# A two-layer hybrid decoder kernel: other orders at its start, in the first mixer's scan and at the change of mixers

## What is computed

```python
h = concatenate([meta, x])
for i in range(2):
    if i == 0:
        h = h + gla_mixer(rms_norm(h, gla_norm), gla_w_in, gla_w_gk, gla_b_gk, gla_head_norm, gla_w_out)
    else:
        h = h + gdn_mixer(rms_norm(h, gdn_norm), gdn_w_in, gdn_conv_w, gdn_a_log, gdn_dt_bias, gdn_head_norm, gdn_w_out)
return rms_norm(h, final_norm)[:, 16:]

# gla_mixer: q, k, v, z, gk_low = split(h @ w_in); gates from gk_low
#   per chunk of 64 tokens: o = (q e^b) S + tril((q e^b)(k e^-b)^T) v ;  S = S * decay + (k e^(b_last-b))^T v
#   return (rms_norm(o, head_norm) * silu(z)) @ w_out
# gdn_mixer: h @ w_in, causal convolution, silu, l2 norm, delta rule in chunks, norm, silu gate, @ w_out
```

## Time and profile before

| | |
|---|---|
| median of 3 runs | 1481.02 us (1479.55 to 1483.16) |
| the profiled execution's own time | 1483.98 us |
| its span | 1482.2 us |
| PE busy | 1433.6 us (97%) |
| PE weight loads | 1201.6 us (81%) |
| DVE busy | 769.2 us (52%) |
| ACT busy | 454.4 us (31%) |
| POOL busy | 376.2 us (25%) |
| mean granted clock of PE | 0.997 |

### The profile page before, as it was taken

One profiled execution on the slowest core, in us unless ns is written; L12 is line 12 of the kernel. 1 busy time (PEld: TensorE's weight loads), 2 busy tenths in 40 slices (PEclk: granted clock), 3 DMA queues, 4 the chain that ended last, 5 costly groups with the idle time before them and its releaser, 6 DMA issues.

```text
span 1482.2 us, 21429 instructions
## 1 busy us (share of the span) xinstructions
PE 1433.6 (97%) x8482; PEld 1201.6 (81%) x8482; DVE 769.2 (52%) x985; ACT 454.4 (31%) x948; POOL 376.2 (25%) x303
## 2 busy tenths in 40 slices
PE   5999999999999999999999998999999999999997
PEld 4777799968788779999999998978887777777776
DVE  4213532233444347654555599989944654444442
ACT  4322741132222234334333632322223631111220
POOL 3122033441111112221221141132434342222200
PEclk9999999999999999999999999999999999999999
DMA  5520144475555223454445232236359794556520
GB/s 177 186 84 29 60 134 158 143 244 175 163 177 174 62 75 100 104 132 112 113 121 193 77 90 72 72 100 184 108 197 248 209 264 138 140 160 165 164 86 29
DMA packets 213996, 200.80 MB, mean 135 GB/s; under 512 B 62856, under 2 KB 177048, under 8 KB 213648
## 3 DMA queue, kind: packets, MB, share of 16 engines
q1 hardware_dynamic: 207312, 187.99, 42.7%
q10 hardware_dynamic: 6592, 11.54, 2.8%
HBM read 132.39 MB, written 67.09 MB: 135 GB/s over the span
## 4 chain that ended last, share of the span: by engine, by line
PE 46%; DVE 11%; issue 2%; ACT 2%; DMA 1%; SPq 1%; DVEq 0%; POOLq 0%; POOL 0%; ACTq 0%
PE banks L2070 12%; PE banks L2137 12%; PE banks L2851 12%; DVE gdn L2363 6%; PE banks L2936 2%; PE banks L2900 2%; PE banks L2905 2%; PE banks L1964 2%; PE banks L1988 1%; DMA gdn<-gdn_v 1%; PE banks L2914 1%; PE banks L2923 1%; PE banks L2864 1%; ACT gdn L2212 1%; ACT gdn L2190 1%
## 5 line engine op out<-in xcount | busy, mean ns | idle before, releaser
L2070 PE MATMUL banks<-hn_hi,gdn 128*128 128x352 f32 x1488 | 300.7, 327 | 0.0
L2070 PEld LDWEIGHTS banks<-hn_hi,gdn 128*128 128x128 f32 x1488 | 242.0, 188 | 4.4 <-issue 2.7
L2363 DVE SCALAR_TENSOR_TENSOR gdn<-gdn,conv_taps,gdn 128x1040 f32<-128x1040 f32 x96 | 169.8, 1768 | 11.0 <-ACT gdn L2198 8.1
L852 PE MATMUL banks<-gdn,hn_hi 128*128 128x512 f32 x528 | 170.5, 405 | 4.9 <-DVE gdn L660 2.3
L2336 POOL TENSOR_TENSOR gdn<-gdn,gdn 128x1024 fp32r<-128x1024 f32 x31 | 95.4, 3078 | 312.8 <-ACT gdn L2173 312.8
L2137 PE MATMUL banks<-gdn,hn_hi 128*128 128x512 f32 x512 | 162.8, 398 | 0.4 <-DVE gdn L2370 0.4
L2070 PE MATMUL banks<-hn_lo,gdn 128*128 128x352 f32 x744 | 158.1, 321 | 0.0
L852 PEld LDWEIGHTS banks<-gdn,hn_hi 128*128 128x128 f32 x528 | 100.2, 192 | 32.0 <-ACT gdn L431 4.9
L2070 PEld LDWEIGHTS banks<-hn_lo,gdn 128*128 128x128 f32 x744 | 125.5, 188 | 0.0
L2137 PEld LDWEIGHTS banks<-gdn,hn_hi 128*128 128x128 f32 x512 | 95.5, 188 | 25.0 <-issue 2.6
L852 PE MATMUL banks<-gdn,hn_lo 128*128 128x512 f32 x264 | 105.2, 398 | 0.0
(11 more groups left out here) (294 smaller groups left out, 2238.5 us busy)
## 6 DMA issues: line engine op xcount, KB each, us to landing
gdn<-in_gdn_w_in SPq DMA_DIRECT2D x32, 512.0 KB, 4.1
gdn<-in_gla_w_in SPq DMA_DIRECT2D x32, 256.0 KB, 5.0
gdn<-in_x SPq DMA_DIRECT2D x16, 512.0 KB, 4.2
gdn_kq<-gdn SPq DMA_DIRECT2D x16, 512.0 KB, 3.8
gdn_v<-gdn SPq DMA_DIRECT2D x16, 512.0 KB, 3.5
gdn<-in_gdn_w_in SPq DMA_DIRECT2D x32, 256.0 KB, 4.3
gdn<-gdn_kq SPq DMA_DIRECT2D x16, 512.0 KB, 3.8
gdn<-gdn_ek SPq DMA_DIRECT2D x16, 512.0 KB, 5.7
```

The costliest lines, as they stand in the source:

```text
L852: mm = pe.matmul(out_bank(g, u, i), h_[:, kt, k], piece_of(w_, q), start=(kt == 0 and e == 0), stop=(kt == KT - 1 and e == 2))
L2070: last = pe.matmul(a[:, b, 0:m], w[n % 2][:, kt, :], x[:, kt, PAD + s:PAD + s + m], start=(kt == 0 and e == 0), stop=(kt == KT - 1 and e = ...
L2363: dve.scalar_tensor_tensor(cv[:, :], xs[:, tap:tap + L], T.cw[:, tap, t:t + 1], cv[:, :], ALU.mult, ALU.add).then_inc(S("ni_conv"), 1)
```

## The change

1. Beginning. SP loads the norm weight as one row (4 KB) and all engines agree on a new order: SP brings token tile 1 ahead of the weight pieces; tile 0's load waits for no memset. PE multiplies a row of ones by the norm row to spread it over the partitions in PSUM; `scale(0)` reads it there, and ACT copies it to SBUF for the others. ACT does a small square ahead of everything. POOL makes two inverse roots, then four lo halves, then two inverse roots; DVE makes all its lo halves ahead of `scale(2)`.
2. First scan tile: DVE's `mask` stands ahead of `weigh(g, 2)`.
3. Tile 0's output projection: only 16 of the 128 columns of the stationary operand carry tokens. The lo half is put into 16 zero columns of the hi half, so 32 products do instead of 48; ACT then copies 32 rows of the result, and DVE adds them in a second instruction (`residual_first`).
4. Steps: `normed` goes behind the next step's `mask`. In the last step PE does the state product ahead of `scores`.
5. Change of mixers: six of the gates' products go ahead of the last `norm_out`, and their second span (24 products) from behind the barrier to ahead of it.

```diff
@@ sync
             def load_x(t):
                 if t == 0:
-                    sp.wait_ge(S("ai_x_zero"), 1)
...
             load_x(0)
-            load_piece(0)
-            sp.dma_start(nw, bc(norm_w, [P, D])).then_inc(S("ai_nw_in"), 16)
+            sp.dma_start(nw_row, norm_w).then_inc(S("ai_nw_in"), 16)
             sp.dma_start(T.k[:, :], T.k_dram).then_inc(S("ai_k_in"), 16)
             load_x(1)
-            load_piece(1)
-            load_piece(2)
+            for q in range(4):
+                load_piece(q)
             load_x(2)
-            for q in range(3, NST):
+            for q in range(4, KT):
                 load_piece(q)
             load_x(3)
-            load_piece(NST)
-            load_piece(NST + 1)
@@ scalar
+            act.wait_ge(S("ai_ones"), 1)
+            act.activation(junk[0:1, 0:P], ones, ACT.Square).then_inc(S("ai_ready"), 1)
+            act.wait_ge(S("ai_ready"), 1)
+            act.wait_ge(S("ai_x_zero"), 1)
             squares(0)
             split(0)
             squares(1)
+            act.wait_ge(S("ai_hn"), 1)
+            for b in range(2):
+                act.activation(nw[:, b * 512:b * 512 + 512], bank[2 + b], ACT.Copy).then_inc(S("ai_nw"), 1)
             high(0)
             split(1)
             split(2)
             high(1)
+            split(3)
             squares(2)
-            for q in range(3, NST):
+            for q in range(4, KT):
                 split(q)
             squares(3)
-            split(NST)
-            split(NST + 1)
             high(2)
@@ vector
-            dve.memset(X[0], 0.0).then_inc(S("ai_x_zero"), 1)
-            dve.wait_ge(S("ai_nw_in"), 16)
+            dve.memset(ones, 1.0).then_inc(S("ai_ones"), 1)
+            dve.memset(X[0][0:PAD, :], 0.0).then_inc(S("ai_x_zero"), 1)
+            dve.wait_ge(S("ai_nw_bc"), 1)
             scale(0)
+            dve.wait_ge(S("ai_nw"), 2)
             scale(1)
...
             B.zero(dve)
+            B.first_mask(dve)
             weigh(g, 2)
             B.first(dve)
@@ tensor
+            pe.wait_ge(S("ai_ones"), 1)
+            pe.wait_ge(S("ai_nw_in"), 16)
+            for b in range(2):
+                mm = pe.matmul(bank[2 + b], ones, nw_row[:, b * 512:b * 512 + 512], start=True, stop=True)
+            mm.then_inc(S("ai_nw_bc"), 1)
             pe.wait_ge(S("ai_k_in"), 16)
             transposes(0)
@@ gla_scan, tensor
+            def out_project_first():
+                pe.wait_ge(S("as_otlo"), 2)
+                for n in range(2):
+                    for kt in range(KT):
+                        for k, w in enumerate((whi, wlo)):
+                            mm = pe.matmul(pY[:, n, :], oT_hi[:, kt, :], w[:, kt, n * 512:(n + 1) * 512],
+                                           start=(kt == 0 and k == 0), stop=(kt == KT - 1 and k == 1))
+                    mm.then_inc(S("as_y"), 1)
...
                 H.products(pe, 0, [1])
+                pe.wait_ge(S("as_su"), GH * (NT - 1))
+                H.products(pe, GATE, [0], range(2))
                 norm_out(s, None)
-                pe.wait_ge(S("as_su"), GH * (NT - 1))
-                H.products(pe, GATE, [0])
+                H.products(pe, GATE, [0], range(2, KT))
+                H.products(pe, GATE, [1])
@@ gla_scan, vector
+            def residual_first():
+                dve.wait_ge(S("as_in_res0"), 16)
+                for n in range(2):
+                    c = slice(n * 512, (n + 1) * 512)
+                    dve.wait_ge(S("as_ylow"), n + 1)
+                    dve.tensor_tensor(hres[0][:, c], pY[:, n, :], hres[0][:, c], ALU.add).then_inc(S("as_hfirst"), 1)
+                    dve.wait_ge(S("as_hfirst"), n + 1)
+                    dve.tensor_tensor(hres[0][96:P, c], hn[96:P, c], hres[0][96:P, c], ALU.add).then_inc(S("as_h1"), 1)
...
                 mask(s)
+                if has2:
+                    normed(s.back().back())
                 if not is_last(s):
                     update(s)
...
-                if has1:
-                    normed(s.back())
@@ gdn_in, tensor
             mm_rest(0, [2])
-            mm_rest(GATE, [1, 2])
+            mm_rest(GATE, [2])
```

More of the change, by code:

```diff
@@ L607, in gpsimd @@
             rsqrt(0)
[L608 removed]
             rsqrt(1)
[L610 removed]
+            for q in range(0, KT, 2):
+                split_lo(q)
             rsqrt(2)
[L612 removed]
             rsqrt(3)
[L614 removed]
             pool.memset(gst[:, :, :], 0.0).then_inc(S("ai_gst0"), 1)
@@ L1161, in scan @@
                     outer(s)
-                wait(pe, S("as_otlo"), s.t * 2)
-                scores(s)
+                if not is_last(s):
+                    wait(pe, S("as_otlo"), s.t * 2)
+                    scores(s)
                 wait(pe, S("as_og"), s.t * 4)
@@ L1169, in scan @@
                 mm.then_inc(S("as_inter"), 1)
+                if is_last(s):
+                    wait(pe, S("as_otlo"), s.t * 2)
+                    scores(s)
                 wait(pe, S("as_at"), s.t + 1)
@@ L1344, in tail @@
             def tail(s):
+                normed(s.back())
                 norm_low(s.back())
@@ L1350, in vector @@
                 zero()
+            elif part == "mask":
+                mask(FIRST)
             elif part == "first":
@@ L1353, in vector @@
             else:
-                low(lambda b: oT_lo[:, 4 * b:4 * b + 4, :], lambda b: oT_hi[:, 4 * b:4 * b + 4, :], 0, "ot", "ot")
+                for b in range(2):
+                    dve.wait_ge(S("as_othi"), b + 1)
+                    o_ = oT_hi[:, 4 * b:4 * b + 4, :]
+                    dve.tensor_tensor(o_[:, :, PAD - 32:P - 32], parts[b][:, :, PAD:P], o_[:, :, PAD:P].bitcast(F32),
+                                      ALU.subtract).then_inc(S("as_otlo"), 1)
                 over_steps(dve, body, tail)
@@ L1384, in body @@
                     norm_high(s.back().back())
+                if has1 and not has2:
+                    for n in range(2):
+                        act.wait_ge(S("as_y"), n + 1)
+                        act.activation(hn[96:P, n * 512:(n + 1) * 512], pY[64:96, n, :], ACT.Copy).then_inc(S("as_ylow"), 1)
                 wait(act, S("as_y"), s.t * 2)
@@ L1702, in product, with products @@
                          start=(kt == 0 and e == 0), stop=(kt == KT - 1 and e == 2))
-    def products(pe, n, spans):
+    def products(pe, n, spans, rows=range(KT)):
         pe.wait_ge(E("gd_hi"), n + 1)
@@ L1707, in products @@
         for b in spans:
-            for kt in range(KT):
+            for kt in rows:
                 for e in range(3):
```

20 lines of the change are left out of this document (10 added, 10 removed).

## The result

| | before | after |
|---|---|---|
| median | 1484.55 us (1479.55 to 1486.52, 6 executions) | 1473.68 us (1472.27 to 1476.45, 6 executions) |
| profiled execution, its span | 1483.98, 1482.2 us | 1473.79, 1472.0 us |
| PE busy | 1433.6 us | 1432.3 us |
| mean granted clock | 0.997 | 0.997 |

The ratio is 0.9928 (0.9917 to 0.9939): faster, by 10.9 us of the medians and 10.2 of the profiled executions, where 13.6 was forecast. The time, 1473.68, lies 0.7 above the range. The kernel before was run three times more beside the changed one, and its median rose from the 1481.02 that I started from to 1484.55.

What follows compares the result with a forecast made beforehand. PE, busy 97% of the span at nearly full clock, was taken as the bound. Gains 4.6 + 4.0 + 0.7 + 2.8 + 3.1 + 1.3 + 0.9 less 3.8 made 13.6 us: 1467.4 from the median 1481.02, range 1462.5 to 1473.0.

Steps and rivals of the forecast that it cites:

- the beginning: Kernel start up to unit 1: the new order starts unit 1 near 24.6, gaining 4.6 us, bounds 2.2 and 7.2.
- My line for being wrong here: At the beginning: if unit 1 starts after 27, the forecast for the beginning is wrong.
- a rival of chance 0.08: Half clock at the new stands behind the barrier costs another 1.4 us: 1468.8, or 1470.2 if also at the beginning.
- First scan tile: First scan tile: with the mask first, PE's stand shrinks to 1.0 and half clock vanishes, gaining 4.0 us (0.8 to 4.0).
- Tile 0: Tile 0's low half shrinks, gaining 0.7 us; its projection drops 16 products, gaining 2.8 net (2.0 to 3.8).
- Steps: Scan steps: `normed` behind the mask saves 0.52 us a step, 3.1 us over six steps.
- Last step: Last scan step: the state product fills the scores' stand but the mask stands exposed, gaining 1.3 us.
- last transposes: Before the last transposes: six products fill the 0.72 us stand, gaining 0.9 us with tails.
- Change of mixers: At the barrier: gate products moved ahead of it cost 3.8 us, not regained behind it; bounds 0 and 3.8.
- the rival of 0.2: Change of mixers: the moved gate products are free, because something behind the barrier hung on them, giving 1463.6; chance 0.2.
- The distance from the taps to silu: Barrier to PE's stand for silu: stays 34.6 us; 31 instead would prove the loss at the change of mixers wrong.
- My line that the barrier's stand of 2.3 us is followed by no half clock: First scan tile term: the barrier's stand served as evidence that a stand of 1.0 should not cost clock.

Runs made afterwards that it cites:

- second profile: The changed kernel profiled once more with no edit, in experiment 1: 1471.63 us, ratio 0.9907 to the kernel before.
- Experiment 7: The changed kernel with piece 6's lo half moved from POOL to DVE (three on POOL, five on DVE): 1470.46 us, ratio 0.9901 to the kernel before.
- experiment 5: The changed kernel with the first scan tile's mask back behind the two weighings: 1477.95 us, ratio 0.9955 to the kernel before.
- experiment 3: The kernel before with only `normed` moved behind the next step's mask: 1479.32 us, ratio 0.9968 to the kernel before.
- experiment 8: The changed kernel with the second mixer's weight loads ahead of tile 8's residual load on SP: 1471.06 us, ratio 0.9908 to the kernel before.
- experiment 2: Gates' second span back behind the barrier in the changed kernel: 1469.28 us, ratio 0.9903; moved alone ahead of it in the kernel before: 1488.23 us, 1.0025.
- experiment 1: The changed kernel run once more with no edit: 1471.63 us, ratio 0.9907 to the kernel before.

## Why the prediction was wrong, and where it was right

The time was forecast as 1467.4 and measured as 1473.68, 6.3 us more. Of these, 3.5 are the median of the kernel before, which rose from 1481.02 to 1484.55 (the anchor, below), and 2.7 are the gain, 10.9 for 13.6. Of the sum's terms one was far off, the beginning.

**The beginning, 4.6 forecast, 2.0 in the profile: the step that failed.** The first part held. The four products of the row of ones took 3.75 us (3.6 forecast), `scale(0)` started at 7.33 (7.3). Then the chain that I had added up from rows of engines working alone fell behind.

`scale(1)` came at 10.06 for 9.7. I had it wait for ACT's copies; it waited for POOL's inverse root of tile 1, behind ACT's square, and ACT makes that square behind its first `split`, which waited for the first weight piece until 7.14:

```profile
7.14 0.63 ACT L428 ACTIVATE gdn<-gdn 128x512 fp32r<-128x512 f32 x1 [2.58 <-DMA gdn<-in_gla_w_in]
```

In the second profile that piece let `split` begin at 6.74, and the copies were the last, as I had said.

`scale(1)` lasted 2.22 us for 1.28, beside POOL's first lo half; in all ten profiles with this beginning it lasted 2.05 to 2.23. With both, unit 0 started at 13.96 for 13.1. I had looked for contention at the mask and not here. The Trainium skill (SBUF — State Buffer, section "Who interferes with whom") has a DVE instruction with two SBUF inputs contend with a GpSimd instruction that reads SBUF; these rows agree, and my sum had no such term here.

POOL's last two lo halves ended at 20.1 for 18.7. They began at 17.09 where I had about 16, since ACT's hi halves follow tile 1, and took 2.99 for 2.56 beside DVE's. Tile 2's root followed 1.5 us behind them for 1.2, and tile 3's stood beside `scale(2)`, one of its instructions taking 1.14 for 0.19; so `scale(3)` ended at 24.9 for 23.5.

Unit 1, forecast at 24.6, started at 25.43 in the second profile. In the first it started at 26.40: 0.4 by the later `scale(1)`, 0.6 by half clock in the transposes ahead of it, and half clock inside unit 1 cost 1.0 more before the first scores.

My line for being wrong here was unit 1 after 27; it came close, and I should have added the clock behind it to that line. Of the 2.6 us missing in the first profile 1.6 are this half clock, which the sum had at nothing and only a rival of chance 0.08 named; the contention and the late start are the other 1.0. Experiment 7 gets 1.1 us back by taking one lo half off POOL.

**First scan tile, 4.0 forecast, 3.9.** Right, and by experiment 5 also as a whole: 0.9955 against 0.9928 is 4.0 us of 1484. There was luck in it: two of the four profiles with the old order stood only 1.5 and 1.6 us, and in such an execution the term would be some 0.2. The mask at 0.7 was right too. DVE's and POOL's rows of the changed kernel:

```profile
317.00 0.75 DVE L1369 COPY_PREDICATED gdn<-consts,banks 128x512 f32<-128x512 int32 x1 [0.24 <-issue]
```

```profile
311.16 12.68 POOL L1007 TENSOR_TENSOR gdn<-gdn,gdn 128x1024 fp32r<-128x1024 f32 x5
```

The mask took 0.75 us though it lies wholly beside POOL's subtractions. That is as the Trainium skill (SBUF — State Buffer, section "Who interferes with whom") has it for an instruction with a single SBUF input.

**Tile 0, 0.7 and 2.8 forecast, 0.6 and 2.8.** Right in both parts: 3.7 by the 16 fewer products, less a stand of 0.85 at step 2's scores where I had said 1.0.

**Steps, 3.1 forecast, 3.6.** The mechanism is right (experiment 3), the size was 0.6 a step for 0.52: the state product and the masked product stood 2.36 us apart before and 1.83 in experiment 3, which is the 0.53 forecast, and from the masked product to the next transposes there were 1.83 and 1.72, 0.1 that I had left out. Last step 1.3 and last transposes 0.9: right.

**The last outputs, not forecast, -0.55.** I had followed SP's queue for the steps and not into the last one, where what is queued behind the residual's load is no token load with 15 us to spare but the next mixer's weights (experiment 8).

**Change of mixers, -3.8 forecast, -3.8.** Right, and the rival of 0.2 is excluded by experiment 2. The distance from the taps to silu was the right thing to watch, and the two stands, forecast at 2 and 1.6, were 1.97 and 1.30.

**Second mixer's scan, 0 forecast, -0.8.** PE waits once, near its start, for DVE, which waits for a tile that comes back from memory:

```profile
1184.70 1.22 DVE L3142 TENSOR_TENSOR gdn<-gdn,banks 128x1024 f32<-128x1024 f32 x1 [8.39 <-DMA gdn<-gdn_v]
```

PE's stand behind it was 0.23 us in the kernel before, 0.94 here, 0.34 in the second profile of the same kernel, and from none to 1.3 in the others. So this is no effect of the change; why the tile's arrival varies was not tried.

**The anchor.** I took the forecast from the median of three executions, 1481.02, and called the profiled one 2.96 us too slow. Of 37 later executions of the kernel before, five lie below 1481 and the median is 1485.09; two of my three were of that rare kind. The five have mean granted clocks of 0.997 and 0.998, and 23 of the other 32 have 0.994 or 0.995. A clock of 0.995 in place of 0.998 over 1480 us is 0.003 x 1480 / 0.5 = 8.9 us at half speed, which cost 4.4: about the distance between the groups. The clock does not sort them all: the profiled execution had 0.997 and took 1483.98, and three of the 37 had 0.997 and took 1483.4 to 1484.3. From the profiled execution's own time the forecast would have been 1470.4 us, for 1473.79 in its first profile and 1471.16 in its second, and a range moved up with it by 3 us would have held 1473.68. The ratio forecast, (1481.0 - 13.6) / 1481.0 = 0.9908, is that of experiment 1 (0.9907) and not that of the first six executions (0.9928).

## What to carry to other kernels

Price what goes beside another engine's work from a row where both run, not from the shortest row of its kind, and do so at every place of the change, not at the one where you first thought of it. Moving work across a barrier pays only if the chain behind the barrier hangs on it: look at which engine ends the first wait there. And take a forecast from the execution that was profiled; if the median of few executions differs from it by as much as a term of the sum, time the kernel before more often ahead of choosing.

## What the runs showed of the hardware

A stand of some 2 us on PE is followed by half clock in some executions of the same code and not in others. Behind the barrier the stand was 2.3 or 2.4 us in all 14 profiles; in six the granted clock then fell to 0.50 (as above), in eight it stayed at 1.00, and the way to silu took 36.0 to 37.6 us in the six and 34.5 to 34.6 in the eight. Near 150 to 155 us all fourteen stood 1.7 to 2.1 us for POOL's lo half, and the clock fell in two, behind 1.8 and 1.9. In the first scan tile, ten stands of 0.95 to 1.33 us with the mask first were followed by no half clock, and neither were two of 1.5 and 1.6; both of 3.4 and 3.6 were.

At the beginning all four profiles with the old order fell to 0.50 for some 3 us between 20 and 27 us, in or behind a stand of 2.1 to 2.8 us for DVE's lo half in the middle of unit 0, and unit 0's later products paid for it. Of the ten with the new order three fell, in unit 0's end or at unit 1. So some of what the new beginning gains is the half clock that it meets less often; no experiment separates that part.

My line that the barrier's stand of 2.3 us is followed by no half clock rested on one profile and was wrong. The Trainium skill (TensorE: Matmul & The Clock Gate, Part 1) has the number of slowed matmuls at a kernel's start vary from run to run for the same kernel. The profiles here show the same behind stands in mid-kernel, so one profile does not tell whether a given stand costs 0 or 1.5 us more.
